# Sparse attention layer: index inputs projected first, rotary rows packed by DMA, logits and first selection moved among the query units

## The reference

```python
q, k, v, qi, ki, wi = jnp.split(h @ w_in, cuts, axis=-1)   # 16 x 64, 4 x 64, 4 x 64, 8 x 64, 64, 8 columns
q, k, qi, ki = (partial_rope(x, cos, sin, 16) for x in (q, k, qi, ki))   # the first 16 of 64 columns turn
...
logits = jnp.einsum('bthd,bsd->bths', qib, ki)             # 8 index heads, one index key
score = jnp.einsum('bths,bth->bts', jax.nn.relu(logits), wib)
score = jnp.where(visible, score, -jnp.inf)                # key before the end of the token's 64-token chunk
_, sel = lax.top_k(score, 64)
...                                                        # softmax attention of 16 heads over the selected keys
```

## Time and profile before

| | us |
|---|---|
| median of 3 runs | 1639.89 |
| lowest, highest | 1637.77, 1641.6 |
| profiled execution, its own time | 1634.39 |
| its span, first to last instruction | 1632.5 |
| granted TensorE clock over the span | 0.999 |

### The profile page before, as it was taken

The page is one execution under the profiler, slowest core; times in us unless marked ns, Lnnn a source line. Parts: engine busy times, 40 slices in busy tenths (PEclk is TensorE's granted clock), DMA queues, the critical chain, the costliest instruction groups (busy, mean ns, idle before and its releaser), DMA issues.

```text
span 1632.5 us, 30999 instructions
## 1 busy us (share of the span) xinstructions
PE 1590.4 (97%) x12663; PEld 1517.9 (93%) x12663; DVE 1011.2 (62%) x1241; ACT 763.9 (47%) x1005; POOL 23.5 (1%) x40
## 2 busy tenths in 40 slices
PE   7989999998999999999999999999999999999999
PEld 5969999998999998999988999989999898889998
DVE  7786665567666546566457666466654656676653
ACT  4345554447555444434346444344443435554443
POOL 0000000013000000000000000000000000000000
PEclk9999999999999999999999999999999999999999
DMA  6702666744256664556623556635566352236573
GB/s 164 183 31 58 179 201 181 197 141 123 83 179 202 182 195 153 181 166 194 181 77 104 180 177 195 168 113 174 178 195 189 103 181 78 79 129 196 189 213 96
DMA packets 347111, 252.70 MB, mean 155 GB/s; under 512 B 32622, under 2 KB 345868, under 8 KB 347036
## 3 DMA queue, kind: packets, MB, share of 16 engines
q1 hardware_dynamic: 345424, 250.00, 51.4%
q10 hardware_dynamic: 1612, 1.64, 0.3%
HBM read 250.58 MB, written 1.05 MB: 154 GB/s over the span
## 4 chain that ended last, share of the span: by engine, by line
PE 86%; DVE 8%; ACT 3%; DMA 2%; issue 1%; SPq 0%; ACTq 0%; DVEq 0%
PE acc L541 26%; PE acc L543 25%; PE acc L542 25%; DVE w_low L1690 2%; ACT w_high L1199 1%; PE acc L566 1%; PE acc L771 1%; PE spare L739 1%; DMA w_raw<-in_ffn_w_dram 1%; PE acc L757 1%; DVE x_state L1900 1%; DVE xg_low L1734 1%; DVE evac_a L1898 1%; PE spare L604 1%; PE spare L566 1%
## 5 line engine op out<-in xcount | busy, mean ns | idle before, releaser
L1690 DVE TENSOR_TENSOR w_low<-w_raw,w_high 128x2048 fp32r<-128x2048 f32 (+2 forms) x222 | 528.5, 2381 | 378.3 <-ACT w_high L1199 378.3
L1199 ACT ACTIVATE w_high<-w_raw 128x2048 fp32r<-128x2048 f32 (+2 forms) x222 | 441.3, 1988 | 612.0 <-PE acc L543 578.3
L541 PE MATMUL acc<-xg_high,w_high 128*128 128x272 f32 (+2 forms) x2320 | 663.4, 286 | 7.6 <-DVE xg_low L1734 4.4
L542 PE MATMUL acc<-xg_low,w_high 128*128 128x272 f32 (+2 forms) x2320 | 654.6, 282 | 0.0
L543 PE MATMUL acc<-xg_high,w_low 128*128 128x272 f32 (+2 forms) x2320 | 654.6, 282 | 0.0
L541 PEld LDWEIGHTS acc<-xg_high,w_high 128*128 128x128 f32 (+1 forms) x2320 | 435.5, 188 | 19.4 <-issue 9.4
L542 PEld LDWEIGHTS acc<-xg_low,w_high 128*128 128x128 f32 (+1 forms) x2320 | 435.5, 188 | 2.4 <-issue 1.7
L543 PEld LDWEIGHTS acc<-xg_high,w_low 128*128 128x128 f32 (+1 forms) x2320 | 435.4, 188 | 0.2
L541 PE MATMUL acc<-hidden_high,w_high 128*128 128x256 f32 (+1 forms) x1216 | 342.2, 281 | 2.6 <-DVE w_low L1690 2.6
L542 PE MATMUL acc<-hidden_low,w_high 128*128 128x256 f32 (+1 forms) x1216 | 341.4, 281 | 0.0
L543 PE MATMUL acc<-hidden_high,w_low 128*128 128x256 f32 (+1 forms) x1216 | 341.4, 281 | 0.0
(11 more groups left out here) (297 smaller groups left out, 1441.7 us busy)
## 6 DMA issues: line engine op xcount, KB each, us to landing
w_raw<-in_ffn_w_dram SPq DMA_DIRECT2D x88, 1024.0 KB, 5.1
w_raw<-in_ffn_w_dram SPq DMA_DIRECT2D x32, 1408.0 KB, 6.9
w_raw<-in_mlp_w_up_dram SPq DMA_DIRECT2D x32, 1024.0 KB, 5.7
w_raw<-in_mlp_w_down_dram SPq DMA_DIRECT2D x32, 1024.0 KB, 5.6
w_raw<-in_attn_w_qkv_dram SPq DMA_DIRECT2D x12, 1024.0 KB, 5.0
w_raw<-in_a_w_in_dram SPq DMA_DIRECT2D x18, 256.0 KB, 4.5
w_raw<-in_a_w_in_dram SPq DMA_DIRECT2D x4, 1024.0 KB, 7.7
w_raw<-in_a_w_out_dram SPq DMA_DIRECT2D x4, 1024.0 KB, 5.2
```

Of the source, the lines that this page charges most:

```text
L541: pe.matmul(dst, high_w, high, start=first, stop=False)
L542: pe.matmul(dst, high_w, low, start=False, stop=False)
L1199: act.activation(whi[slot(c)][:, 0:SIZES[c]], raw[c % 2][:, 0:SIZES[c]], ACT.Copy).then_inc(S["w_high"], 1)
L1690: dve.tensor_tensor(wlo[slot(c)][:, s], raw[c % 2][:, s], whi[slot(c)][:, s].bitcast(F32), ALU.subtract)\
```

## The change

Everything is in the sparse layer.

- **Order of units.** Index queries (0, 1), index key and weights (2), values (3), keys (4), queries (5 to 8).
- **Weights.** A query chunk is loaded by two DMAs of 128 columns instead of four of 64, and reordered by the splits: two operations of 128x8x128 on ACT and on DVE in place of one of 128x2048 (`four_apart_pairs`).
- **Rotary.** `turn_rope`, its constant matrix and `rope` are gone. `projected` evacuates each unit straight into a tensor of five tiles per group: index (4 query tiles and the key), first heads (4 query tiles and a key tile), last heads (the same). For a group, ACT issues four DMAs (`pack`) that copy the rotary rows, 8 partitions x 5 tiles x 256 tokens of 1 KB runs each, into 80 partitions of a small tensor; DVE turns them with four operations (`rope_packed`: two on 80x512, two on 80x256); ACT issues four DMAs back (`unpack`). Three groups make 24 DMAs of 40 KB, SBUF to SBUF.
- **Logits and selection.** Pairs 0 to 3 of the logits stand after tiles 2 to 5 of unit 6, pairs 4 to 7 after tiles 4 to 7 of unit 7. The relus, the weighted sums (`weigh`) and the eight selection rounds (3, 4 and 1) stand between the splits of units 6 to 8.
- **Attention.** The scores of piece 0 wait for the key group's return, those of piece 4 for the last group's. The last group is turned by DVE within piece 1, and its four return DMAs are issued by ACT there. Dummies before the first mask: 4 instead of 16; in the first pieces 2, 1 instead of 4, 4; behind unit 8 none instead of 7.

```diff
-            for j in range(4):
-
-                h = 8 * (j // 2) + 2 * (j % 2)
-                load_chunk(c + 3 + j, w, parts=[(x * HD, HD) for x in (h, h + 4, h + 1, h + 5)])
-            load_chunk(c + 7, w[:, :, Q_COLS:Q_COLS + KV_COLS])
-            load_chunk(c + 8, w[:, :, Q_COLS + KV_COLS:Q_COLS + 2 * KV_COLS])
+            load_chunk(c + 3, w[:, :, Q_COLS + KV_COLS:Q_COLS + 2 * KV_COLS])
+            load_chunk(c + 4, w[:, :, Q_COLS:Q_COLS + KV_COLS])
+                load_chunk(c + 5 + j, w, parts=[(h * HD, 2 * HD), ((h + 4) * HD, 2 * HD)])
...
-            for j in range(9):
-                split(g.c0 + j + 2)
+            def pack(j, tiles, to, signal):
+                act.wait_ge(S["dve_evac"], g.r0 + j + 1)
+                for c, s in HALVES:
+                    act.dma_start(packed(to, c, s), turning(tiles, c, s)).then_inc(S[signal], 16)
+            def unpack(tiles, src, roped, signal):
+                act.wait_ge(S[roped], 1)
+                for c, s in HALVES:
+                    act.dma_start(turning(tiles, c, s), packed(src, c, s)).then_inc(S[signal], 16)
...
+            for j in range(3):
                 split(g.c0 + j + 2)
+            pack(2, indexA, packI, "idx_packed")
+            split(g.c0 + 5)
+            split(g.c0 + 6)
+            unpack(indexA, packI, "idx_roped", "idx_back")
             copy_v([(sp[0][:, i, 0:KV_COLS], vA[:, i, :]) for i in range(2)])
+            split(g.c0 + 7)
+            relus(0)
+            split(g.c0 + 8)
+            pack(6, first_heads, packK, "key_packed")
+            relus(4)
+            split(g.c0 + 9)
+            unpack(first_heads, packK, "key_roped", "key_back")
+            split(g.c0 + 10)
+            pack(8, last_heads, packQ, "query_packed")
```

More of the change, by code:

```diff
@@ L70 @@
 C_INVB = C_INVA + 1
-C_RA = C_INVB + 1
-C_RB = C_RA + P
+C_RB = C_INVB + 1
 C_CHUNK = C_RB + P
@@ L108, in constants @@
     c[:, C_ID:C_ID + P] = np.eye(P)
[L109 to L112, removed]
     for head in range(0, P, B_ROPE):
@@ L724, in turn_values, with attention @@
                     ins.then_inc(S["v_turned"], 1)
-            def attention(pieces, scores, prob_tiles, values, probs_by, idle=(), early=0, values_in=0, mask=None):
+            def attention(pieces, scores, prob_tiles, values, probs_by, idle=(), early=0, values_in=0, mask=None, before=None):
                 s0, t0, o0, e0 = n.get("s_read"), n.get("pt_ready"), n.get("o_read"), n.get("exp_done")
@@ L735, in make_scores @@
                 def make_scores(p):
+                    if before is not None:
+                        before(*pieces[p])
                     if p >= 2:
@@ L837, in key_and_weights, with index_logits, beside @@
                 return cols(c, a, a + (P if m == 0 else IDX_HEADS)), (P if m == 0 else IDX_HEADS)
-            wide(g, 2, META, SEQ, tiles=key_and_weights)
[L840 to L847, removed]
+            def index_logits(first, k0):
+                def beside(k):
+                    if not k0 <= k < k0 + 4:
+                        return
+                    q = first + k - k0
+                    i, m = q // 4, q % 4
+                    if q == 0:
+                        pe.wait_ge(S["idx_back"], 16 * 4)
+                        pe.wait_ge(S["v_ready"], n.add("v_ready", 2))
+                        pe.wait_ge(S["wi_ready"], 1)
+                    if q >= 2:
+                        pe.wait_ge(S["idx_relu"], q - 1)
+                    for c in range(2):
+                        r = slice(c * HD, (c + 1) * HD)
+                        ins = pe.matmul(sp[q % 2][:, c, 0:(i + 1) * P], indexA[r, m, i * P:(i + 1) * P],
+                                        indexA[r, 4, 0:(i + 1) * P], start=True, stop=True)
+                    ins.then_inc(S["idx_full"], 1)
+                return beside
+            wide(g, 2, META, SEQ, tiles=key_and_weights)
+            wide(g, 3, META, SEQ)
             pe.wait_ge(S["wi_in"], 1)
@@ L1198, in split @@
                     return
+                if c in head_pairs:
+                    for dst, src in zip(four_apart_pairs(whi[slot(c)]), loaded_pairs(raw[c % 2])):
+                        ins = act.activation(dst, src, ACT.Copy)
+                    ins.then_inc(S["w_high"], 1)
+                    return
                 act.activation(whi[slot(c)][:, 0:SIZES[c]], raw[c % 2][:, 0:SIZES[c]], ACT.Copy).then_inc(S["w_high"], 1)
@@ L1372, in copy_v, with attention @@
                     act.activation(d, pieces, ACT.Copy).then_inc(S["v_ready"], 1)
-            def attention(pieces, keys, slots, outs, first=None):
+            def attention(pieces, keys, slots, outs, first=None, beside=None):
                 s0, t0, o0 = n.get("s_read"), n.get("pt_full"), n.get("o_full")
@@ L1402, in attention @@
                         exps(p)
+                    if beside is not None:
+                        beside(p)
                     if outs and p >= 3:
@@ L1685, in split @@
                     for dst, src, high in zip(query_tiles(wlo[slot(c)]), query_parts(raw[c % 2]), query_tiles(whi[slot(c)])):
+                        ins = dve.tensor_tensor(dst, src, high.bitcast(F32), ALU.subtract)
+                    ins.then_inc(S["w_low"], 1)
+                    return
+                if c in head_pairs:
+                    for dst, src, high in zip(four_apart_pairs(wlo[slot(c)]), loaded_pairs(raw[c % 2]),
+                                              four_apart_pairs(whi[slot(c)])):
                         ins = dve.tensor_tensor(dst, src, high.bitcast(F32), ALU.subtract)
@@ new lines, in weigh @@
+            def weigh(first):
+                for q in range(first, first + 4):
+                    i, m = q // 4, q % 4
+                    nk = (i + 1) * P
+                    dve.wait_ge(S["idx_relu"], q + 1)
+                    for c in range(2):
+                        add_to = cst[:, C_CHUNK + i * P:C_CHUNK + i * P + nk] if m == 0 and c == 0 else \
+                            score[:, i, 0:nk]
+                        ins = dve.scalar_tensor_tensor(score[:, i, 0:nk], Sm[q % 2][:, c, 0:nk],
+                                                       wiA[:, i, 2 * m + c:2 * m + c + 1], add_to, ALU.mult, ALU.add)
+                        if c == 0:
+                            link(ins)
+                    ins.then_inc(S["idx_read"], 1)
+                    dve.wait_ge(S["idx_read"], q + 1)
```

171 lines of the change are left out of this document (100 added, 71 removed).

## The result

The changed kernel took 1652.2 us (median of 13 executions, 1641.6 to 1665.4) where the kernel before took 1640.0 (13, 1634.0 to 1644.1). The ratio is 1.008, interval 1.006 to 1.010: slower, by 12 us, where 8.8 us of gain were forecast. Against the earlier trace rows PE is busy for as large a share of a longer span, so the page's first part shows nothing amiss. It is the granted clock in 40 slices, tenths of full speed; it was 9 throughout before.

What follows compares the result with a forecast made beforehand. It took a serial stretch of DVE and ACT ahead of attention, with PE waiting behind dummies, as the bound. 12.9 - 1.4 - 2.2 - 0.2 - 0.3 = 8.8 us saved, so 1639.9 - 8.8 = 1631.1 us; range 1627 to 1637.5.

Steps and rivals of the forecast that it cites:

- Part 1: PE's projection units: unit 6 ends at 66.2 us, unit 8 at 79.7, with the logits done and no gain in PE's end.
- Part 2: DVE's chain from chunk 8's split to the mask: sum 20.8 us, mask ends at 89.2 against 102.13, gain 12.9 us.
- Part 3: SBUF-to-SBUF transfers: 0.5 us an issue, landing after 2.9 us; the first two round trips cost nothing.
- Part 4: Clock behind unit 8: PE idles from 79.7 to 85.9 us and the level is low then; -1.4 us, bounds 0 and -2.3.
- with the level rising on the way, as it did at the start: First scores and four dummies behind unit 8: done at 90.3 us instead of 91.1 at the low level throughout.
- Part 5: Inside attention: last group's rotary -2.2 us, its transfer -0.2 (bounds 0 and -4.1), ACT's blocked queue -0.3.
- 10.0 among the signs: Attention: sign of a right forecast, the maximum of piece 4 at 10 us after that of piece 0.
- the sum's three terms: Attention, pieces 0 to 4: losses of 2.2 us for the rotary, 0.2 for the transfer, 0.3 for ACT's queue.
- The 0.3 us for ScalarE's blocked queue: Attention: ACT's queue stands 4 us behind the return issues while DVE turns the group and selects; 0.3 us added.
- the clock also falls within attention: Rival: two pieces of PE's work at the low level, up to 3.8 us more, 1634.9 us; 0.17 with an equally dear wait.
- slower: Rival: from 7.2 us a transfer the gain is gone, at 9 us 7.4 us slower, 1647.3 us; chance 0.06.
- a wait of 2.3 us in mid-run lowers nothing: The longest mid-run wait of PE, 2.3 us, didn't lower the clock; by it alone the sum would be 1.4 us larger.

Runs made afterwards that it cites:

- e1_gap8: The changed kernel with seven dummy matmuls of 512 columns behind unit 8, nothing else: 1646.0 us, ratio 1.0045 to the kernel before.
- e2_both: The changed kernel with dummies in both gaps, behind unit 8 and in attention's first pieces: 1632.5 us, ratio 0.9962 to the kernel before.
- e7_return_sp: `e2_both` with the last group's four return transfers issued on SyncE's queue instead of ScalarE's: 1627.4 us, ratio 0.9950 to the kernel before.
- e4_before_bare: The kernel before with only its dummies removed or cut as in the changed kernel: 1651.7 us (four executions), ratio 1.0074.
- e13_cover: `e8_mask_first` with five dummies of 256 columns behind the mask: 1631.7 us, ratio 0.9959 to the kernel before.
- e10_all: `e8_mask_first` with five dummies behind the mask, return transfers on SyncE's queue and dummies in the second layer's attention: 1629.3 us, ratio 0.9968.
- e6_burst: The changed kernel with four dummies of 512 columns ahead of piece 4's turned probabilities: 1642.4 us, ratio 1.0023 to the kernel before.
- e8_mask_first: The changed kernel with dummies in both gaps and DVE's split of weight chunk 10 moved behind the first block's mask: 1631.7 us, ratio 0.9957.

## Why the prediction was wrong, point by point

**Part 1** held as far as it mattered. Unit 6 was read by DVE at 67.3 (forecast 66.2 for its end), the last unit ended at 81.5 (86.53 - 5.07, forecast 79.7), still ahead of DVE's chain; PE had no pause from 55 to 80 us, so no wait stood ahead of the first logits.

**Part 2** held, in part by luck: the chain ran without a gap, but from 69.33 instead of 68.4, 0.9 us late behind unit 6, and took 20.0 us instead of 20.8. The two cancel, and the mask ended at 89.32, forecast 89.2.

**Part 3** held, with two errors that cancel: an issue took 0.72 us instead of 0.5 (2.86 us for four), a landing 2.4 instead of 2.9. First issue to last landing was 96.56 to 101.2, 4.6 us against 4.4. The rule on the number of engines that the prediction cites stands in the Trainium skill's page "DMA: Bandwidth & Descriptors" under "Why a DMA increments its semaphore by 16 and not by 1"; no run here shows how many engines a copy used. This is the chain's row of the last landing:

```profile
98.75 2.44 DMA a_query_key<-a_query_rotary
```

**Part 4** held for what it priced: the low level at 85.9 delays the first maximum by 1.4 us (91.82, against 90.39 in `e1_gap8` with that gap covered; forecast -1.4). Its step "with the level rising on the way, as it did at the start" did not: the scores, the four dummies (3.78 us, 1.99 in `e1_gap8`) and the mask's matmuls all ran at 0.50, and the level rose at 92.2 us, behind them. From the first score to the mask's matmuls 4.4 us passed (86.53 to 90.90), just the forecast (85.9 to 90.3), so the size was right and its reason wasn't.

**Part 5** is where it failed. With the level up its sum is right: maxima 0 and 4 are 10.3 us apart in `e2_both`, forecast 10.0 among the signs and 10.3 by the sum's three terms, before 7.6; piece 4's maximum is 8.8 us early, as summed, and `a_out` starts 8.0 us early. That it is just 8.8 owes something to chance: the 1.4 us for the level aren't lost in `e2_both`, whose first maximum still comes at 91.32 and not at 89.9, since its dummies stand in PE's way. At clocks of 0.998 and 0.999 four executions of `e7_return_sp` take 1626.5 to 1627.6 us, where the kernel before took 1635.7 and 1637.0 on the same chip: 8 to 10 us saved. By medians less is left. The three kernels that only put dummies back take 1630.9, 1632.5 and 1632.5, near the forecast of 1631.1, but the kernel before was at 1637.7 and 1638.1 beside them, so they save 6.8, 5.3 and 5.6 us of the 8.8. Some of the rest goes where the level falls in the second layer, as the profile of `e2_both` shows.

The failed step is another. It took it that the level, once risen, stays up between small matmuls with waits in them, and that was never costed. The 0.3 us for ScalarE's blocked queue priced VectorE's delay alone, not that PE would stand for 2.25 us with nothing behind its one dummy. The rival that names it, "the clock also falls within attention", priced it by two pieces of block 0, 3.8 us, on the unspoken ground that a busy PE has the level back soon. It stayed low for all pieces from the second on and for the transposes behind them: 95.6 to 153.7 us. It cost 17.3 us from piece 4 on and 5.8 at the end, 23 instead of 3.8, which would have turned this rival into "slower". It got 0.17 with the wrong price; no range of mine reached 1652. The rival called "slower" had 0.06 and the right sign, but for transfers of more than 7.2 us, and the one measured landed in 2.4.

The reasoning error is in what I took the earlier trace rows and the clock of 1.00 before to show: that a wait of 2.3 us in mid-run lowers nothing. That wait itself stood behind five dummies of 512 columns, at a granted clock of 1.00:

```profile
836.20 4.45 PE L566 MATMUL spare<-constants,ones 128*128 128x512 f32 x10
842.99 0.35 PE L1026 MATMUL acc<-w_high,xg_high 128*128 128x256 f32 x1 [2.34 <-DVE xg_low L1734]
```

For this wait no run took the dummies away. For attention `e4_before_bare` did, and there 14 us hang on them. The Trainium skill ("TensorE: Matmul & The Clock Gate", Part 1) has the low level as the default that activity releases. The runs agree as far as the default goes (0.50 behind the idleness at unit 8), not in that being busy is enough: from 104 to 120 us PE was busy for 16.00 of 16.00 us at 0.50. I had read the page's rule as a price for one gap instead of for everything behind it.

What stays open: why one or two of twelve executions of the covered kernels `e13_cover` and `e10_all` are still long, what ends the falls in the second layer, and which property of PE's work around 92 to 98 us decides. Best by median is `e7_return_sp`, 1627.4 us over six executions; `e2_both` has no execution of twelve above 1636.0. Both keep the change and beat both kernels; six and twelve executions are too few to tell them apart, or to say that `e2_both` has less risk than the kernels with one or two long executions in twelve.

## What to carry to other kernels

Ahead of removing a dummy, or of letting a busy engine wait, ask what runs behind it, not how long the gap is: the price is nearly half of the time that PE then spends at the low level, here 23 of the 58 us up to the next dense stretch. Look at the granted clock by stretches of a few us before any other view of the profile when a kernel slows down with PE at 97% busy. And where a change moves work away from PE, put cover in its place in the same edit; thirteen matmuls of 128 columns decided 20 us.

## What I had not expected of the hardware

Being busy isn't enough to regain the level: attention's mix of transposes, 64-row scores and 64-column products ran for nearly 50 us at 0.50, busy for 47.55 of 48 us, and sixteen transposes in a row (3.67 us) left it there, while the dummies of 512 columns that start at 108.06 in `e6_burst` had raised it by 111. Yet the same mix holds the level once it is up (104 to 124 us in `e2_both`, all at 1.00). In `e1_gap8` the mix itself raised it, at 141.9 us, behind 48 us at the low level, and in `e8_mask_first` four dummies of 128 columns among the mix had it back at 94.5 us, 3 us behind its fall. In `e1_gap8` it had fallen behind waits of no more than 1.14 us; `e2_both` has one of 1.13 us at the same place and held it, with more dummies behind. And it differs from execution to execution of one kernel, which lie up to 24 us apart; by what isn't known.
